# Attention scores as three reduced-precision products in place of one full-precision product, with the low parts made on VectorE

## The reference

```python
q = partial_rope(q.reshape(bsz, s, N_HEADS, HEAD_DIM), cos, sin)
k = partial_rope(k.reshape(bsz, s, N_KV_HEADS, HEAD_DIM), cos, sin)
...
logits = jnp.einsum('bnqhgd,bnkhd->bnhgqk', qb, kb,
                    preferred_element_type=jnp.float32) * (HEAD_DIM ** -0.5)
...
probs = jax.nn.softmax(jnp.concatenate([logits, sink_col], axis=-1), axis=-1)[..., :-1]
out = jnp.einsum('bnhgqk,bnkhd->bnqhgd', probs.astype(v.dtype), vb)
```

## Time and profile before

| | |
|---|---|
| median of three runs | 950.02 us (949.94 to 950.05) |
| span of the profiled execution, first to last instruction | 948.2 us |
| own device time of the profiled execution | not given apart; the median is 1.8 us over the span |
| TensorE matmul busy | 928.1 us, 98% of the span |
| VectorE busy | 724.2 us, 76% |
| ScalarE busy | 576.6 us, 61% |
| TensorE in the chain that ended last | 97% |
| score products (L809) | 64 records, 15.1 us of busy time |
| mean granted TensorE clock | 0.997 of full speed |

### The profile page before, as it was taken

The page is one execution under the profiler, slowest core; times in us unless marked ns, Lnnn a source line. Parts: engine busy times, 40 slices in busy tenths (PEclk is TensorE's granted clock), DMA queues, the critical chain, the costliest instruction groups (busy, mean ns, idle before and its releaser), DMA issues.

```text
span 948.2 us, 12500 instructions
## 1 busy us (share of the span) xinstructions
PE 928.1 (98%) x5068; PEld 800.5 (84%) x5068; DVE 724.2 (76%) x971; ACT 576.6 (61%) x730; POOL 1.4 (0%) x9
## 2 busy tenths in 40 slices
PE   4999999999999999999999999999999999999996
PEld 3898888988888888888889889888888888888885
DVE  5887898787867867767867688888878676866755
ACT  4578889764356644555345889887435564545540
POOL 0000000000000000000000000000000000000000
PEclk9999999999999999999999999999999999999998
DMA  9546444584485655566453544456756656555621
GB/s 330 159 160 200 135 156 156 185 303 166 156 266 183 200 195 178 194 201 207 157 162 122 204 159 157 132 179 192 261 177 216 229 185 203 189 179 196 202 90 45
DMA packets 118457, 174.62 MB, mean 184 GB/s; under 512 B 3968, under 2 KB 78976, under 8 KB 117888
## 3 DMA queue, kind: packets, MB, share of 16 engines
q1 hardware_dynamic: 118256, 173.79, 55.1%
q10 hardware_dynamic: 144, 0.03, 0.0%
HBM read 172.76 MB, written 1.05 MB: 183 GB/s over the span
## 4 chain that ended last, share of the span: by engine, by line
PE 97%; DVE 1%; DMA 1%; ACT 0%; SPq 0%; issue 0%; DVEq 0%
PE ring L541 16%; PE ring L543 16%; PE ring L542 16%; PE ring L594 9%; PE ring L590 9%; PE ring L593 5%; PE ring L591 5%; PE misc L543 5%; PE misc L541 5%; PE misc L542 4%; PE misc L771 2%; PE misc L809 1%; PE misc L829 1%; PE ring L714 1%; DMA sb_hb<-in_w_in_dram 1%; PE ring L725 1%
## 5 line engine op out<-in xcount | busy, mean ns | idle before, releaser
L1245 DVE TENSOR_TENSOR sb_w_lo<-sb_raw,sb_w_hi 128x2048 fp32r<-128x2048 f32 x138 | 294.7, 2148 | 67.5 <-ACT sb_w_hi L925 67.4
L925 ACT CAST sb_w_hi<-sb_raw 128x2048 fp32r<-128x2048 f32 x138 | 246.2, 1795 | 16.1 <-DMA sb_raw<-in_w_proj_rnn_dram 3.9
L541 PE MATMUL ring<-sb_w_hi,sb_x_both 128*128 128x512 f32 x272 | 108.1, 397 | 0.0
L594 PE MATMUL ring<-sb_x_both,sb_w_hi 128*128 128x512 f32 x272 | 107.6, 396 | 0.0
L590 PE MATMUL ring<-sb_x_both,sb_w_hi 128*128 128x512 f32 x272 | 107.5, 395 | 0.0
L543 PE MATMUL ring<-sb_w_hi,sb_x_both 128*128 128x512 f32 x272 | 106.1, 390 | 0.0
L542 PE MATMUL ring<-sb_w_lo,sb_x_both 128*128 128x512 f32 x272 | 106.0, 390 | 0.0
L593 PE MATMUL ring<-sb_x_both,sb_w_lo 128*128 128x256 f32 x272 | 75.7, 278 | 0.0
L591 PE MATMUL ring<-sb_x_both,sb_w_lo 128*128 128x256 f32 x272 | 75.4, 277 | 0.0
L541 PE MATMUL ring<-sb_x_both,sb_w_hi 128*128 128x256 f32 x256 | 73.0, 285 | 0.0
L543 PE MATMUL ring<-sb_x_both,sb_w_lo 128*128 128x256 f32 x256 | 72.4, 283 | 0.0
(11 more groups left out here) (223 smaller groups left out, 2085.8 us busy)
## 6 DMA issues: line engine op xcount, KB each, us to landing
sb_raw<-in_w_in_dram SPq DMA_DIRECT2D x40, 1024.0 KB, 5.2
sb_raw<-in_w_up_dram SPq DMA_DIRECT2D x34, 1024.0 KB, 5.2
sb_raw<-in_w_down_dram SPq DMA_DIRECT2D x18, 1024.0 KB, 4.9
sb_raw<-in_w_proj_attn_dram SPq DMA_DIRECT2D x8, 1024.0 KB, 5.0
sb_raw<-in_w_proj_rnn_dram SPq DMA_DIRECT2D x8, 1024.0 KB, 5.1
sb_hb<-in_w_up_dram SPq DMA_DIRECT2D x8, 1024.0 KB, 5.2
sb_raw<-in_w_out_dram SPq DMA_DIRECT2D x6, 1024.0 KB, 6.0
sb_raw<-in_w_ple_gate_dram SPq DMA_DIRECT2D x6, 1024.0 KB, 5.7
```

What stands on the lines that cost most here:

```text
L541: nc.tensor.matmul(dst, lhs[0], rhs[0], start=first, stop=False)
L594: last = nc.tensor.matmul(bank_of(*key), hi[:, cols], x_both[:, k + 1], start=False, stop=k + 2 == KT)
L925: nc.scalar.copy(hi_at[home][:, at], raw_at[home][:, at]).then_inc(s_hi_part, 1)
L1245: nc.vector.tensor_tensor(lo_at[home][:, 0:size], raw_at[home][:, 0:size], hi_at[home][:, 0:size].bitcast(F32), ALU.subtract).then_inc(s_s ...
```

## The change

`qkT` becomes an fp32r buffer, so that ScalarE's copy rounds and what it holds is the high part. VectorE makes the low part of each pair of heads, from the transposed values in `misc` minus `qkT`: for query pairs into `a_lo`, for the two key heads into rows 0 and 4 of `a_hi`. Each score product becomes three fp32r products. Everything that waited for ScalarE's copies (`qk_ready`) and that overwrites `misc` or reads scores operands now waits for the low parts (`qk_lo_ready`). Of VectorE's five low parts, four stand at i = 2 ahead of `gate_input`, and the fifth behind `conv` and ahead of `softmax_max`.

```diff
-        qkT = sb("qkT", [P, QK_HEADS, SEQ])
+        qkT = sb("qkT", [P, QK_HEADS, SEQ], F32R)
...
+        def qk_lo_of(pair):
+            first = 2 * pair
+            if first < HEADS:
+                return a_lo[:, first:first + 2, :]
+            return a_hi[:, 0:HEADS, :].rearrange("p (g i) s -> p g i s", g=KV_HEADS)[:, :, 0, :]
...
                     if i == 4:
-                        pe.wait_ge(s_qk_ready, value("qk_ready", l, 4))
+                        pe.wait_ge(s_qk_lo_ready, value("qk_lo_ready", l, 4))
...
                 if r == 0:
-                    pe.wait_ge(s_qk_ready, value("qk_ready", l, 4))
+                    pe.wait_ge(s_qk_lo_ready, value("qk_lo_ready", l, 4))
                 else:
                     if r == TT:
-                        pe.wait_ge(s_qk_ready, value("qk_ready", l, 5))
+                        pe.wait_ge(s_qk_lo_ready, value("qk_lo_ready", l, 5))
                     pe.wait_ge(s_exp_done, value("exp_done", l, 5 * r))
+                keys = [qkT[:, HEADS + g, :], a_hi[:, GROUP * g, :]]
                 for i in range(GROUP):
-                    last = nc.tensor.matmul(misc[:, i // 2, SEQ * (i % 2):SEQ * (i % 2 + 1)],
-                                            qkT[:, GROUP * g + i, b * P:(b + 1) * P], qkT[:, HEADS + g, :],
-                                            start=True, stop=True)
+                    head = GROUP * g + i
+                    last = three(misc[:, i // 2, SEQ * (i % 2):SEQ * (i % 2 + 1)],
+                                 [x[:, head, b * P:(b + 1) * P] for x in (qkT, a_lo)], keys, True, True)
                 last.then_inc(s_scores, 1)
...
-                    pe.wait_ge(s_qk_ready, value("qk_ready", l, 5))
+                    pe.wait_ge(s_qk_lo_ready, value("qk_lo_ready", l, 5))
...
+            def qk_lo(l, steps):
+
+                for i in steps:
+                    dve.wait_ge(s_qk_ready, value("qk_ready", l, i + 1))
+                    pair = QK_PAIRS[i]
+                    nc.vector.tensor_tensor(qk_lo_of(pair), misc[:, min(i, 3), :].rearrange("p (h s) -> p h s", h=2),
+                                            qkT[:, 2 * pair:2 * pair + 2, :].bitcast(F32),
+                                            ALU.subtract).then_inc(s_qk_lo_ready, 1)
...
                     split_to(l, f"rg{i // RNN_BLOCKS}", i % RNN_BLOCKS)
+                    if name == "ga0":
+                        qk_lo(l, range(4))
                     gate_input(l, i)
                     split_to(l, name, 1)
                     if i + 2 < 2 * RNN_BLOCKS:
                         conv(l, i + 2)
+                    if name == "ga0":
+                        qk_lo(l, [4])
                     if 2 <= i <= 5:
                         softmax_max(l, i - 2)
```

More of the change, by code:

```diff
@@ L238 @@
 PER = dict(
-    ln_step=2 * TT * LN_STEPS, ln_norm=4 * TT, x_turned=3 * 4, x_hi=3 * 4, x_ready=3 * 4,
+    qk_lo_ready=5, ln_step=2 * TT * LN_STEPS, ln_norm=4 * TT, x_turned=3 * 4, x_hi=3 * 4, x_ready=3 * 4,
     rope_step=6, qk_turned=5, qk_ready=5,
@@ L347, in hybrid_encoder @@
         s_qk_ready = sem("qk_ready")
+        s_qk_lo_ready = sem("qk_lo_ready")
         s_scores = sem("scores")
```

## The result

| | before | with the change |
|---|---|---|
| median of 21 runs | 950.14 us (949.93 to 951.33) | 951.30 us (951.11 to 952.32) |
| ratio | | 1.0013, 95% interval 1.0007 to 1.0019 |
| span of the profiled execution | 948.2 us | 950.4 us |
| its own time | not given apart | 952.2 us |
| TensorE busy | 928.1 us | 928.2 us |

The change makes the kernel 1.2 us slower (951.30 against 950.14), a ratio of 1.0013, which lies within the 0.2% that the prediction took as no change. The median came out at the predicted 951.3 us. Of the five executions of the one-product kernel further down, one took 1151.4 us at a mean clock of 0.754 and is left out of its ratio.

The account below looks back on a forecast made before the run. TensorE was taken to bound the kernel: two pauses of 1.8 us less eight rounds shorter by 0.29 us, 3.6 - 2.3 = +1.3 us, gave a median of 951.3 us. The forecast's own range was 951.0 to 951.9 us.

Parts of the forecast that it names:

- TensorE sets the time in the mixer: Mixer stages: time saved or paused on TensorE moves the total; VectorE or ScalarE work costs nothing until TensorE waits.
- A shorter round, 0.29 us: Scores: twelve fp32r products take 1.44 us where a round took 1.73; eight rounds save 2.3 us.
- The rival at 3/4 of the old round: Scores: reduced products cost 3/4 of the full round, 1.30 us; gain 3.5 us, time 950.1 us; chance 0.06.
- The pause, 1.8 us twice: Transposes ahead of the scores: TensorE waits for VectorE's four low parts, 1.8 us a layer, 3.6 us together.
- The sum, +1.3 us: Whole kernel: 3.6 us lost less 2.3 us gained, span 948.2 to 949.5 us, median 951.3 us.
- VectorE's backlog taken up by its idle time: VectorE behind the four low parts: idle 1.14 and 1.10 us absorb the added 2.4 us within the same i.
- The fifth low part at nothing: Ahead of softmax_max of round 0: its 0.6 us is covered by a 2.6 us margin; uncovered, 0.7 us a layer.
- The clock rival: Pause ahead of the scores: TensorE's clock falls, 1.9 us of work doubles twice, +3.8 us, 955.1 us; chance 0.04.
- The wait hidden, 947.7: Transposes: the four low parts are done by 93.81, only the 2.3 us gain remains, 947.7 us; chance 0.04.

Follow-up runs that it names:

- e2_one_product: Against the change, each score is one fp32r product, high by high, in place of three, the wait kept: 946.95 us, ratio 0.9966.
- e4_early: Against the change, the four low parts stand ahead of the gate input's low part and the weight item: 948.99 us, ratio 0.9986.
- the two kernels with one product: e2_one_product, and the same kernel with the fifth low part moved behind softmax_max: 946.95 us and 945.49 us.
- The pause alone: Against the change, each score is one full-precision product again, the low parts and the wait for them kept: 953.68 us, ratio 1.0039.
- the kernel with both edits: e4_early with the fifth low part also moved behind softmax_max of round 0: 947.79 us, ratio 0.9977.
- e3_late: Against the change, the four low parts stand behind gate_input instead of ahead of it: 959.78 us, ratio 1.0101.

## Why the prediction was right

- **TensorE sets the time in the mixer: right.** Every edit moved the time by what it did to TensorE's list, apart from `e4_early` and the two kernels with one product, where TensorE came to wait for something else.
- **A shorter round, 0.29 us: right.** Between like products of the two traces it is 0.28 to 0.31 us, and 2.4 us for all eight by the difference of two kernels. The chain's pieces for round 0 give 1.42 us where the gates block had 1.44. The rival at 3/4 of the old round would have had 1.30 us. The measured round is 0.82 of the old one. The Trainium skill, "FP8 and Floating Point Precision", section "TensorE Precision Notes", counts four passes for true FP32; here that count is not a price, since one reduced product costs 0.12 of 0.43 us and not a quarter.
- **The pause, 1.8 us twice: right.** 1.70 us by starts, with 0.05 more for the first transposes (0.65 instead of 0.60 us): 1.75. The pause alone measured 3.5 us, so the term of 3.6 was 0.1 too high. The price of a low part came from the attention low part, and L1434 has it: starts 0.60 us apart, 0.68 us for one.
- **The sum, +1.3 us: right, and the hundredth is luck.** The change measured +1.16. The kernel before came out at 950.14 us instead of the 950.02 that the forecast started from, and this made up for the difference.
- **VectorE's backlog taken up by its idle time: right**, to the hundredth at the weight item (96.60).
- **The fifth low part at nothing: right for this kernel** (951.19 against 951.30), and the price if the cover goes was put at 0.7 us a layer; it is 0.6. But I checked its margin at the transposed probabilities (2.6 us) and not at the place where it ends first, the read-out of ga1 ahead of the gates block of i = 4. There the margin was 0.6 us before the change (in `e4_early` TensorE is 0.6 early, ScalarE 0.6 late, and 0.6 is lost), and it only held because TensorE came late.
- **The clock rival: wrong here, and right as a mechanism.** In the pause of the change the clock stayed up. In the pause of 4.0 us it fell and cost 1.5 us a layer; I had put 1.9.
- **The wait hidden, 947.7: wrong for the change.** It is what the kernel with both edits gives, 947.8, since the low parts then are ready at 93.8.

## What to carry to other kernels

A change that makes the bound engine's work cheaper, but needs a product of another engine first, is decided by where that product stands in the other engine's list: here 2.4 us of gain stood against 3.5 us of waiting, and moving the four low parts ahead and the fifth back turned +1.2 into -2.4 us. Price a pipelined engine's work by the distance from start to start, and a wait by the end of the last instruction in the list ahead of it. Check the margins again after a success, too: what a pause covered comes up once the pause is gone.

## What the runs showed of the hardware

- A full-precision product of 256 columns is two records and 0.43 us; three reduced ones are 0.355 us (1.42 us for twelve), each with its own weight load.
- TensorE's granted clock stayed at 2.4 GHz over pauses of 1.5 us and fell to 1.2 GHz after pauses of 4.0 us, at the restart or 0.5 us behind it; it cost 1.5 us each time, in both layers alike. Between the two lengths nothing was tried at this place. At the end of the kernel before, where TensorE was done at 940.4, the window from 942 to 943 has a mean clock of 0.85, which is 0.3 us at half speed, so there it fell some 2.3 us after the last work.
- In some executions eight products of the first query unit of layer 0 take 3.60 us instead of 2.11, nearly twice as long; in the profiled pair that makes most of the 1 us between the two groups. The windows print a clock of 1.00 there, but this early it proves nothing: the trace of the kernel before has its first clock record at 14.3 us and that of the change at 20.4 us, and the print is 1.00 wherever there is none. In both, the first transposes take 1.09 and 1.05 us, where the same form later takes 0.60. So the likely reading is that TensorE still ran at 1.2 GHz, for 6 us longer in one than in the other. `e2_one_product` and `e3_late`, both profiled 1.2 to 1.4 us late at the start, have their first record at 20.8 us; the others, from 14.6 to 17.0 us, have these products at 2.1 us. What decides when the clock rises stays open.
